# Depthwise taps two to a weight tile on 64-row halves, and a Mamba decay spread by two products, in a two-block network

## The reference

```python
def conformer_conv_module(u, w_pw1, b_pw1, dw_w, dw_b, ln_g, ln_b, w_pw2, b_pw2):
    h = u @ w_pw1 + b_pw1
    a, g = jnp.split(h, 2, axis=-1)
    h = a * jax.nn.sigmoid(g)
    h = causal_depthwise_conv(h, dw_w, dw_b)      # y[t, c] = sum_k w[k, c] * h[t - 30 + k, c] + b[c]
    h = jax.nn.silu(layernorm(h, ln_g, ln_b))
    return h @ w_pw2 + b_pw2
```

## Time and profile before

| | |
|---|---|
| median of 3 runs | 2535.39 us (2534.23 to 2536.71) |
| the profiled execution | 2539.79 us, its span 2538.0 us |
| mean granted clock of TensorE | 0.987 of full speed |
| PE busy | 2468.8 us, 97% of the span |
| DVE, ACT, POOL busy | 1264.3 us, 920.7 us, 1045.5 us |
| conformer's depthwise stage | about 913 to 988 us in the trace |

### The profile page before, as it was taken

The page is one execution under the profiler, slowest core; times in us unless marked ns, Lnnn a source line. Parts: engine busy times, 40 slices in busy tenths (PEclk is TensorE's granted clock), DMA queues, the critical chain, the costliest instruction groups (busy, mean ns, idle before and its releaser), DMA issues.

```text
span 2538.0 us, 31751 instructions
## 1 busy us (share of the span) xinstructions
PE 2468.8 (97%) x13107; PEld 2007.4 (79%) x13107; DVE 1264.3 (50%) x2010; ACT 920.7 (36%) x1527; POOL 1045.5 (41%) x480
## 2 busy tenths in 40 slices
PE   8999998999999999999999999999999999999999
PEld 6778887788887887788888788888777678788887
DVE  7777676554445598564433542223466645322222
ACT  3434443222223377222223232223466642122221
POOL 4334334544444310744444544444322234544443
PEclk9999999999999999999999999999999999999999
DMA  4112222454442210454432223223111123223322
GB/s 156 50 59 75 67 75 67 148 184 159 155 159 92 84 50 10 141 179 161 166 112 96 89 97 100 94 97 99 60 59 59 59 67 100 83 93 99 100 93 90
DMA packets 70992, 252.72 MB, mean 100 GB/s; under 512 B 8000, under 2 KB 8512, under 8 KB 70848
## 3 DMA queue, kind: packets, MB, share of 16 engines
q1 hardware_dynamic: 58752, 210.27, 25.5%
q10 hardware_dynamic: 12096, 40.42, 4.4%
HBM read 248.56 MB, written 2.10 MB: 99 GB/s over the span
## 4 chain that ended last, share of the span: by engine, by line
PE 88%; DVE 8%; ACT 3%; issue 1%; POOL 0%; ACTq 0%; DMA 0%; DVEq 0%; POOLq 0%
PE ps L507 26%; PE ps L509 26%; PE ps L508 26%; PE ps L556 1%; PE ps L549 1%; PE ps L587 1%; PE ps L740 1%; DVE arena L1425 1%; PE ps L742 1%; PE ps L741 1%; DVE XL L1434 1%; DVE tmpm L1425 1%; PE ps L655 1%; DVE XL L1425 1%; PE ps L525 1%
## 5 line engine op out<-in xcount | busy, mean ns | idle before, releaser
L2138 POOL TENSOR_TENSOR WL<-raw,WH 128x1024 fp32r<-128x1024 f32 x391 | 951.2, 2435 | 1231.9 <-ACT WH L928 1225.0
L507 PE MATMUL ps<-XH,WH 128*128 128x512 f32 x3160 | 1251.2, 396 | 34.1 <-DVE XL L1425 15.8
L508 PE MATMUL ps<-XL,WH 128*128 128x512 f32 x3160 | 1238.2, 392 | 0.0
L509 PE MATMUL ps<-XH,WL 128*128 128x512 f32 x3160 | 1237.9, 392 | 0.0
L507 PEld LDWEIGHTS ps<-XH,WH 128*128 128x128 f32 x3160 | 598.9, 190 | 169.9 <-issue 17.9
L509 PEld LDWEIGHTS ps<-XH,WL 128*128 128x128 f32 x3160 | 598.2, 189 | 126.6
L508 PEld LDWEIGHTS ps<-XL,WH 128*128 128x128 f32 x3160 | 599.2, 190 | 124.4 <-issue 2.2
L928 ACT ACTIVATE WH<-raw 128x1024 fp32r<-128x1024 f32 x306 | 322.4, 1057 | 734.2 <-PE ps L509 607.5
L1425 DVE SCALAR_TENSOR_TENSOR arena<-arena,ps 128x512 f32<-128x512 f32 x88 | 60.4, 686 | 518.7 <-ACT arena L1124 505.6
L2136 POOL CAST WH<-raw 128x1024 fp32r<-128x1024 f32 x85 | 95.1, 1118 | 238.9 <-PE ps L509 218.0
L1425 DVE SCALAR_TENSOR_TENSOR h<-ps,der,h 128x512 f32<-128x512 f32 x104 | 77.3, 750 | 160.3 <-PE ps L509 160.1
(11 more groups left out here) (250 smaller groups left out, 1827.6 us busy)
## 6 DMA issues: line engine op xcount, KB each, us to landing
raw<-in_w SPq DMA_DIRECT2D x394, 512.0 KB, 3.4
arena<-in_w_mod ACTq DMA_DIRECT2D x72, 512.0 KB, 4.4
o_out<-h SPq DMA_DIRECT2D x8, 256.0 KB, 2.0
h<-in_x SPq DMA_DIRECT2D x4, 256.0 KB, 7.6
h<-in_x ACTq DMA_DIRECT2D x4, 256.0 KB, 6.5
raw<-in_w SPq DMA_DIRECT2D x2, 256.0 KB, 4.1
arena<-in_c ACTq DMA_DIRECT2D x1, 512.0 KB, 4.5
vec<-in_vec ACTq DMA_DIRECT2D x1, 295.5 KB, 9.9
```

What stands on the lines that cost most here:

```text
L507: e.matmul(b, wh, XH[:, x, :], start=i == 0, stop=False)
L508: e.matmul(b, wh, XL[:, x, :], start=False, stop=False)
L509: p = e.matmul(b, wl, XH[:, x, :], start=False, stop=i == len(slots) - 1)
L2138: e.tensor_tensor(lo, x, hi.bitcast(F32), SUB).then_inc(*did(("split", c)))
```

## The change

(1) Tiles 3 to 7 now have 24, 30, 30, 30 and 30 of their 31 taps on PE (144 instead of 92). Two taps share one 128x128 weight tile, and these 72 tiles are laid out on the host as nine more chunks of the weight stream (139 to 147; all later chunks move up by nine), whose high part is rounded on POOL. A tile holds tap k+1 on its diagonal and tap k in the entries 64 columns off, so that the result of tap k stands in the other 64 partitions, one token early. Each of the three products is made as two matmuls, one for each half of the rows, into two banks. ACT's `late_taps(i)` copies the 64x511 corner of each bank to its place in `cv[i]`; DVE's chain waits for that, does the taps left, and adds the two banks' other halves with 64x512 instructions, which also let the banks go. ACT makes no diagonals any more. The order of PE's token sums among the taps is written anew, and DVE finishes chains 0 to 5 (`until(5)`) ahead of the mean.

(2) `head(n)` makes two 512-column products in the fast type: a column of `sel` (the sum of the identity's four 32-column blocks) times the high and the low part of the decays, laid out block by block over 512 columns in `acd`. These are filled with zeros at the start (DVE), copied by ACT in step `dt` and by DVE in step `dec`.

(3) The mixer's `gb[0:2]` use other buffers, with a wait on ACT for two earlier products.

```diff
-TAPS = [0, 0, 0, 14, 18, 22, 22, 16]
+
+TAPS = [0, 0, 0, 24, 30, 30, 30, 30]
...
-CHUNK0 = {"mamba": 0, "f0": 57, "conv": 123, "f1": 147, "f2": 213, "mix": 279, "f3": 329}
+CHUNK0 = {"mamba": 0, "f0": 57, "conv": 123, "taps": 139, "p2": 148, "f1": 156, "f2": 222, "mix": 288, "f3": 338}
...
+    if CHUNK0["taps"] <= c < CHUNK0["p2"]:
+        return False
...
-                    w.wait_ge(*at("acs"))
-                    for c in range(4):
-                        p = e.matmul(b[:, c * P:(c + 1) * P], ident[:, 32 * c + n:32 * c + n + 1].broadcast_to([P, P]), acs,
-                                     start=True, stop=True)
-                    p.then_inc(*did(("sum", "p", n)))
+                    w.wait_ge(*at("acd", 1))
+                    one_head = sel[:, n:n + 1].broadcast_to([P, P])
+                    e.matmul(b, one_head, acd[0], start=True, stop=False)
+                    e.matmul(b, one_head, acd[1], start=False, stop=True).then_inc(*did(("sum", "p", n)))
...
+                halves = (slice(0, 64), slice(64, 128))
+
+                def taps(i, k0, k1):
+
 
                     if k0 == 0:
-                        tap_bank[i] = bank(("tap", i), CB)
-                    b = tap_bank[i]
+                        tap_banks[i] = bank(("tap", i, 0), (0, 2, 4)), bank(("tap", i, 1), (1, 3))
                     a0 = by_pe.index(i) * W
                     w.wait_ge(*at("xp_lo", i))
-                    for k in range(k0, min(k1, TAPS[i])):
-                        n = sum(TAPS[:i]) + k
-                        gh, gl = diags[n % len(diags)]
-                        w.wait_ge(*at("diag", i, k))
-                        e.matmul(b, gh, fh[:, a0 + k:a0 + k + T], start=k == 0, stop=False)
-                        e.matmul(b, gh, fl[:, a0 + k:a0 + k + T], start=False, stop=False)
-                        p = e.matmul(b, gl, fh[:, a0 + k:a0 + k + T], start=False, stop=k == TAPS[i] - 1)
-                        p.then_inc(*did(("tap", i, k), *((("sum", "tap", i),) if k == TAPS[i] - 1 else ())))
+                    for k in range(k0, k1, 2):
+                        wh, wl, c, ends = weights(("taps", 0, i, k))
+                        last = k == TAPS[i] - 2
+                        for n, (d, x) in enumerate(((wh, fh), (wh, fl), (wl, fh))):
+                            for r, b in zip(halves, tap_banks[i]):
+                                p = e.matmul(b, d[r, :], x[r, a0 + k + 1:a0 + k + 1 + T], start=k + n == 0, stop=last and n == 2)
+                        if ends or last:
+                            p.then_inc(*did(*([("used", c)] if ends else []), *([("sum", "tap", i)] if last else [])))
 
                 CB, XB = (0, 1, 2, 3, 4), (5, 6, 7)
-                tap_bank = {}
+                tap_banks = {}
...
-                taps(3)
-                taps(4)
+                taps(3, 0, 24)
+                taps(4, 0, 30)
+                taps(5, 0, 8)
                 b = bank(("mean", 0), XB)
-                for i, (t, k0, k1) in enumerate(((5, 0, 8), (5, 8, 16), (5, 16, K), (6, 0, 6))):
-                    taps(t, k0, k1)
+
+                def mean_of_first(i):
                     w.wait_ge(*at("cv", i))
-                    p = token_sums(b, cv[i], one, i == 0, i == 3)
-                p.then_inc(*did(("sum", "mean", 0)))
-                taps(6, 6, 14)
+                    return token_sums(b, cv[i], one, i == 0, i == 3)
+
+                taps(5, 8, 18)
+                mean_of_first(0)
+                taps(5, 18, 30)
+                mean_of_first(1)
+                taps(6, 0, 8)
+                taps(6, 8, 18)
+                mean_of_first(2)
+                taps(6, 18, 24)
+                mean_of_first(3).then_inc(*did(("sum", "mean", 0)))
+                taps(6, 24, 30)
                 w.wait_ge(*at("mean", 0))
                 spread(("mw", 0), small("mean", 0), XB)
-                taps(6, 14)
+                taps(7, 0, 6)
                 mean, var = bank(("mean", 1), XB), bank(("var", 0), XB)
                 for i in range(4):
-                    taps(7, 2 * i, 2 * i + 2)
+                    taps(7, 6 + 4 * i, 10 + 4 * i)
                     squares_of(i)
                 for i in range(4, NT):
-                    taps(7, 4 * i - 8, 4 * i - 6)
+                    if i < 6:
+                        taps(7, 4 * i + 6, 4 * i + 10)
                     mean_of(i)
-                    taps(7, 4 * i - 6, 4 * i - 4)
                     squares_of(i)
...
+                        for c in range(4):
+                            d = A(acd[0][32 * c:32 * c + 32, c * P:(c + 1) * P], acs[32 * c:32 * c + 32, :], ACT.Copy)
+                        d.then_inc(*did(("acd", 0)))
...
-                def diagonals():
-                    for i, k in tap_list:
-                        n = sum(TAPS[:i]) + k
-                        gh, gl = diags[n % len(diags)]
-                        if n >= len(diags):
-                            w.wait_ge(*at("tap", *tap_list[n - len(diags)]))
-                        w.wait_ge(*at("wlo"))
-                        A(gh, ident, ACT.Copy, scale=V("dw_w", 8 * k + i))
-                        A(gl, ident, ACT.Copy, scale=wlo[:, 8 * k + i:8 * k + i + 1]).then_inc(*did(("diag", i, k)))
-                        yield
-
-                diagonal = diagonals()
-
-                def diagonals_to(n):
-
-                    while built[0] < min(n, len(tap_list)):
-                        next(diagonal)
-                        built[0] += 1
-
-                built = [0]
+                def late_taps(i):
+
+                    w.wait_ge(*at("sum", "tap", i))
+                    A(cv[i][0:64, 1:T], ps("tap", i, 0)[64:128, 0:T - 1], ACT.Copy)
+                    A(cv[i][64:128, 1:T], ps("tap", i, 1)[0:64, 0:T - 1], ACT.Copy).then_inc(*did(("late", i)))
...
+                for i in by_pe[:-1]:
+                    late_taps(i)
+                sqrt_table()
+                for i in range(NT):
+                    square(i)
                     if i == 5:
-                        diagonals_to(len(diags))
-                first = sum(TAPS[:7])
-                for i in range(NT):
-                    diagonals_to(first + (2 * i if i < 4 else 4 * i - 8) + len(diags) - 1)
-                    if i == 0:
-                        sqrt_table()
-                    square(i)
+                        late_taps(7)
...
+                for a in acd:
+                    d = TS(a, junkm[:, 1:2].broadcast_to([P, T]), 0.0, None, MUL)
+                d.then_inc(*did(("junk",)))
...
+                    elif what == "dec":
+                        w.wait_ge(*at("acd", 0))
+                        for c in range(4):
+                            rows, cc = slice(32 * c, 32 * c + 32), slice(c * P, (c + 1) * P)
+                            TT(acd[1][rows, cc], acs[rows, :], acd[0][rows, cc].bitcast(F32), SUB)
+                        TT(sel_f, ident[:, 0:32], ident[:, 32:64], ADD).then_inc(*did())
+                        own()
+                        TT(sel_f, sel_f, ident[:, 64:96], ADD).then_inc(*did())
+                        own()
+                        TT(sel, sel_f, ident[:, 96:128], ADD).then_inc(*did(("acd", 1)))
...
+                    n = 0
+                    if TAPS[i]:
+                        for _ in range(12 if i == 3 else 0):
+                            yield
+                        w.wait_ge(*at("late", i))
+                    else:
+                        TS(cv[i], x, V("dw_w", 8 * (K - 1) + i), V("dw_b", i), MUL, ADD).then_inc(*did())
+                        n = did.n
+                        yield
+                    for k in range(TAPS[i], K if TAPS[i] else K - 1):
                         w.wait_ge(s_dve, n)
                         late = K - 1 - k
                         d = STT(cv[i][:, late:T], x[:, 0:T - late], V("dw_w", 8 * k + i), cv[i][:, late:T], MUL, ADD)
                         yield
                     if TAPS[i]:
                         w.wait_ge(s_dve, n)
-                        w.wait_ge(*at("sum", "tap", i))
-                        TT(cv[i], cv[i], ps("tap", i), ADD).then_inc(*did(("cv", i), ("free", "tap", i)))
+                        for half in range(2):
+                            r = slice(64 * half, 64 * half + 64)
+                            STT(cv[i][r, :], ps("tap", i, half)[r, :], V("dw_b", i)[r, :], cv[i][r, :], ADD, ADD).then_inc(
+                                *did(("free", "tap", i, half), *((("cv", i),) if half else ())))
...
-                until(3)
-                more(14)
+                until(5)
...
+        if name == "taps":
+            for s in range(2):
+                w[c, lanes, j * P + (lanes + 64 * s) % P] = g["cv_dw_w"][i, cols + 1 - s, rows * P:(rows + 1) * P]
+            continue
```

More of the change, by code:

```diff
@@ L24 @@
 K = 31
-TAPS = [0, 0, 0, 14, 18, 22, 22, 16]
+TAPS = [0, 0, 0, 24, 30, 30, 30, 30]
 EPS, EPS2 = 1e-5, 1e-6
-TILES = (41 * 8 + 16 * 8) + 4 * (44 * 8 + 22 * 8) + (16 * 8 + 8 * 8) + (34 * 8 + 2 * 8 * 4 + 8 * 8)
```

(24 more changed lines are left out.)

12 lines of the change are left out of this document (3 added, 9 removed).

## The result

The changed kernel takes **2552.10 us** (median, 2550.68 to 2554.37) against 2535.98 for the kernel before: ratio 1.0066, 95% interval 1.0050 to 1.0082. It is slower by 16.1 us where 6.9 were forecast; direction and range (2530 to 2556) held, the size did not, and the forecast's own narrower range (2537 to 2548) was left.

The account below looks back on a forecast made before the run. PE was taken to lead the chain (88%), with the depthwise stage balanced between PE and DVE. Terms -11.2 + 2.5 - 1.5 + 4.8 + 3.0 + 9.3 = +6.9 us on 2535.4 gave 2542, range 2530 to 2556 (own 2537 to 2548).

Parts of the forecast that it names:

- Part 1: Taps on PE: a pair of 64-row matmuls takes 0.235 us, 216 pairs 50.8 us, 13.6 less on PE.
- (c): Taps on PE: a pair costs 1.17 matmuls, 0.272 us, +5.0, 2547 (about 2552 by the skill's ratio); chance 0.10.
- (d): Taps on PE: the row halves take turns after all, +50 us on the taps, 2581 us; chance 0.08.
- Rival (b): Mamba: heads pay in full (-16.6) and their set-up is hidden, without collisions too: 2526.6 us, faster; chance 0.12.
- part 6: Mamba heads: cheaper head products save 11.2 us after later waits; new set-up in the decays costs 2.5.
- Parts 2 and 3: Depthwise stage: new PE waits and longer tail leave -1.5 us with the taps' saving; POOL's subtracts delaying DVE add 4.8.
- Rival (a): Depthwise stage: runs without POOL collision and without clock drop, 2534.5 us, not slower; chance 0.25.
- Part 4: Clock: PE's longer bank waits bring half-clock stretches, 1.5 to 6.0 us; one long one taken, +3.0.
- Part 5: Second pointwise product (p2): four weight roundings ahead of the first gate, ending at 10.25 instead of 0.95, 9.3 us later.
- part 3: Depthwise stage: DVE taps with both tensors in SBUF wait for POOL's subtracts of tap weights, +4.8 us.

Follow-up runs that it names:

- e2: The changed kernel with the Mamba heads as they were before (four fp32 products of 128 columns, no set-up of decays): 2553.61 us, ratio to before 1.0068.

## Why the prediction was right, and where it was not

*Part 1 held.* The halves of a pair start together and the next pair comes 0.23 us later (rows above; 4.37 us for 18 pairs after, 0.243 each with the start), so L879 against a full matmul was a fit neighbour, and the pair cost no more than the full matmul itself. The 3.07 of four that the Trainium skill gives ("TensorE: Matmul & The Clock Gate", "Measured speedup vs the span model") does not describe two halves of fp32r: by it a pair was estimated at 0.306 us, 5.5 us for those 18, and 4.37 were measured. Rivals (c) and (d) fall. Rival (b) needed the heads in full, and falls with part 6.

*Parts 2 and 3 held in every wait.* Forecast and measured: tile 5's bank 8.3 and 7.3 us; tile 6's 3.3 and 3.9; the mean 2.35 and 2.3; the tail, from the last tap product to the last squares, 6.6 and 6.4 (982.0 to 988.45; over the 2.2 of before 6.6 is 4.4 more, put down as 4.5). POOL's subtract was put at 4.8 us; without it the waits fell by 3.6. Rival (a), no collision, falls with the rows of 2.2 us.

*Part 4 was too small, by count.* One half-clock stretch was charged, 3.0 us; there were three in the tap stage, a fourth at the last squares and a longer one at p2. What the clock lacked in the three, times PE's busy time in their rows, is 4.2 us, an estimate; in the fourth it is 2.9. The stage: first tap to the last squares takes 74.4 us before (913.1 to 987.45) and 81.8 after (906.6 to 988.45), +7.5 against +6.3.

*Part 5 held in its mechanism.* The gate comes 10.28 us after the first rounding (forecast 10.25), 9.3 more than before. But p2's wait is 11.9 us where 13.5 were forecast, and taking the roundings out of the way shortened the stretch by only 7.8. That nothing covers them was not quite so: the spread products in front now run at half clock (3.78 us instead of 2.13), and DVE comes later. The whole stretch is 10.3 us longer (17.7 against 7.4): 7.8 are the roundings, 2.5 what stays without them. That the conformer's sum came out at 16.7 against 15.6 is in part luck, by the 1.2 us up to the first tap.

*Part 6 is the step that failed*, and with it the size. The sum had the heads at -11.2 and their set-up at +2.5, a net of -8.7; the profiles show -2.9 against the old heads and the medians -1.5. The set-up was sized right as far as the profiles tell (1.2 to 2.4). Four things were wrong in the heads.

A pair saves 0.86 us, not 1.04: its four products take 0.43 + 3 x 0.23 in the chain after, the first longer than the rest:

```profile
101.52 0.43 PE ps L590
101.95 0.23 PE ps L591
102.19 0.23 PE ps L590
102.42 0.23 PE ps L591
```

The pairs followed by PE's work alone were counted as saved in full; the chain of before showed PE-bound pieces there, but not how little DVE lagged: the waits grew from 9.2 to 16.6 us.

DVE's time was taken as given, and it grew. The groups by line (57 to 405 us) have the same 32 products of DVE with all tensors in SBUF, with the old heads (e2) and after:

```profile
L1598 DVE TENSOR_TENSOR arena<-arena 128x512 f32<-128x512 f32 x32 | 27.9, 872 | 0.0
```

```profile
L1604 DVE TENSOR_TENSOR arena<-arena 128x512 f32<-128x512 f32 x32 | 36.8, 1149 | 0.0
```

The three kernels with the old heads have 27.9 us each, the nine with the new ones 36.7 to 36.8. Among the 32 products, 7 last over 0.8 us with the old heads and 14 after, and each of these ends 0.54 to 0.55 us after an instruction of POOL: it is the collision that part 3 priced for the taps and part 6 left out. It also made most of the longer wait of the first group. There the last pair's two products took 0.68 and 0.93 us before (the second is the first row here), and after 1.37 and 2.22, 2.0 more; POOL's subtract stands beside the last of them:

```profile
126.52 0.93 DVE L1600 TENSOR_TENSOR arena<-arena 128x512 f32<-128x512 f32 x1
```

```profile
125.00 1.37 DVE L1604 TENSOR_TENSOR arena<-arena 128x512 f32<-128x512 f32 x1
126.90 2.22 DVE L1604 TENSOR_TENSOR arena<-arena 128x512 f32<-128x512 f32 x1
...
125.91 2.67 POOL L2154 TENSOR_TENSOR WL<-raw,WH 128x1024 fp32r<-128x1024 f32 x1
```

Why the two engines meet more often now is argued only: POOL starts on a chunk when PE lets a slot go, so an earlier PE moves POOL's work against DVE's. No run moved POOL's work in Mamba, so how much of the 7.4 us of waits is the collisions stays open.

And the longer wait of the first group lowered the clock, 2.2 us that the sum didn't have. Groups two to four gave 7.0 of the 8.4 that three quarters of 11.2 would be; the first group gave +4.0 (1.2 + 0.6 + 2.2), where the sum had -0.3. With the measured heads in place of the forecast ones, the sum would have been 2535.4 + 15.6 - 1.5 = 2549.5. Of the 2.6 us that are left, 1.1 are the conformer's and 0.6 the median of before, which moved from 2535.4 to 2536.0.

## What to carry to other kernels

Work taken off an engine is only gained where that engine is the last to arrive, and a wait that grows can cost twice, since the clock can fall behind it (0.52 for 7 us here): look at the distance to the next wait, not at the engine's share of the chain. An engine that comes earlier can also move the work of the others against each other: a collision priced in one stage (POOL's subtract beside DVE) is to be looked for in every stage whose timing shifts. When weights are moved into a stream with a few slots, ask whose early loading they push out: here three of the next stage's first four chunks had stood ready, and after the change all four were rounded ahead of the gate. A bank, a slot or a chunk that is let go by an instruction at the end of another engine's queue is worth a look before its work is: one other bank for tile 5 was 15.7 us.

## What the runs showed of the hardware

Two 64-row matmuls on different row halves run side by side even when two others of the first one's half stand between them in the queue (they start 10 ns apart in the median of 216 pairs). A DVE instruction whose tensors all lie in SBUF waits for a POOL subtract or cast under way to end (0.73 becomes 2.2 us beside a subtract and 1.13 beside a cast, each ending 0.54 to 0.55 us after POOL's), while one with a PSUM operand goes on at 0.72 beside the subtract. And 2.8 us of products that nobody reads brought the next landmark 2.2 us closer, by keeping the granted clock at 1.00 instead of 0.52 through 7 us.
